# Forgetting attention: the second head of each unit takes its query tiles from long to short, with every projection group in one PSUM bank

## The chip, the cores and the metric

The kernel runs on one core of one Trainium2 chip. The metric is the device time of one execution in microseconds; the median of three runs stands for a kernel.

## What is computed

A decoder block over 1024 tokens of width 1024, in float32: an RMS norm, one wide projection, two kinds of attention, a gated sum of both, an output projection, and then an MLP. The change touches the forgetting attention, eight heads of width 64:

```python
s = jnp.einsum('bqhd,bkhd->bhqk', q_blk, k) * scale
s = s + jnp.transpose(F_blk, (0, 2, 1))[..., None] - F_k
mask = k_pos[None, :] <= q_pos[:, None]
s = jnp.where(mask[None, None], s, NEG_INF)
p = jax.nn.softmax(s, axis=-1)
return jnp.einsum('bhqk,bkhd->bqhd', p.astype(v.dtype), v)
```

The mask is causal. A tile of 128 queries, number i of 8, needs the key tiles 0 to i, that is i + 1 of them. The first query tile is the shortest, with one key tile, and the last is the longest, with eight.

## The kernel before

Every engine has its own instruction list, written out by hand; semaphores tie the lists together. Inputs are split into a high and a low part of float32r, and a projection is three products (high by high, high by low, low by high).

**Units and steps.** The attention is worked in ten units `t` of two heads. Units 0 to 5 are the dilated attention, units 6 to 9 (`N_DIL` to `N_DIL + 3`) the forgetting attention; they are called F0, F1, F2 and F3 here. A unit has 16 steps `s`, one per query tile of one head, and a step's number over the whole program is `G = 16 t + s`. Two steps are a block `B`, with two neighbouring query tiles of one head. `head_of` alternates the heads from block to block. `query_tile` gives both heads their tiles in rising order, so that the number of key tiles runs 1, 2, 1, 2, 3, 4, 3, 4, 5, 6, 5, 6, 7, 8, 7, 8 over the steps 0 to 15.

**What a step does on each engine.**

- TensorE (`mixer_steps`, L1235 on) issues `scores(G)` (L1184) into `PS[G % 2]`, a first part of a projection group (L1141), the transposes of the probabilities of step G - 1 (L1196), and the other two parts of the projection. At odd steps `values` (L1217) of block (G - 3)/2 follows. At the steps 1 and 2, four transposes of the values follow (L1230), which use the same two half banks of `PS[2]` as the transposes of the probabilities.
- VectorE runs `maxes(G)` (L2208: bias and row maximum), the subtraction `probs_lo(G - 1)` (L2215), at even steps `outs` (L2229) ahead of `maxes` and `query_lo` behind it, `values_lo` (L2196) at the steps 1 and 2, and side work: halves of `split_lo` (L2110) for projection weights, `k_stack` (L2181), and at step 7 `normalise` (L2245). In F0 it also merges the dilated groups (L2239).
- ScalarE starts a step with `raw_evacuate` (L1587) for each projection group that ended in the step before, then at even steps `out_part` (L1679), then `query_hi` (L1640), `probs_hi(G - 1)` (L1664), `exps(G)` (L1654), at the steps 1 and 2 `values_hi` (L1647), and last the side work of the step: `split_hi` (L1547) by the table `HI_STEPS` or `k_stack` (L1627) by `K_HI_STEPS`.

The lists are in program order on each engine. So an evacuation at the head of step G stands behind all that ScalarE does in step G - 1, side work included. `HI_STEPS` puts a weight cast at step 2 of F1 and F3 and at step 8 of F1, among others; `K_HI_STEPS` puts a key cast at step 8 of F2.

**Projection groups.** While a forgetting unit is worked, the projections that a later unit needs are computed in between: `group_steps` gives five groups of 24 products to each of F0, F1 and F2, at the steps 0 to 2, 3 to 5, 6 to 8, 9 to 11 and 12 to 15, and four to F3, of four steps each. A group accumulates in a half of one PSUM bank pair. Mostly this is the upper half of `PS[3]`. One group per unit, named in `SECOND_BANK`, takes the upper half of `PS[0]` instead; it lies idle in the steps 0 to 7, where the scores of even steps need at most the lower half. In F0, F1 and F2 that is the group of the steps 3 to 5; in F3 it is the group at the steps 0 to 3, and `scores` waits at step 8 until that bank is emptied. `evacuated(u, g)` says how many evacuations must be done before a group may start (the wait on `raw_out` in `project`, L1138): a group that changes the bank need not wait for the one just before it.

```python
def psp(u, g):
    other = g % 2 if u <= N_DIL else (u, g) in SECOND_BANK.values()
    return (PS[0] if other else PS[3])[:, HALF:2 * HALF]
```

**Around the mixers.** Before F0 stands the combination of the dilated groups. After step 15 of F3 two more steps drain the last block, and then TensorE goes on with the gate projections (L1315), while VectorE and ScalarE start forming the operands of the gate products once the last `values` is done.

Of the kernel before, what the change touches and what calls it, by code (L numbers as in the profile page):

```python
# [32 lines left out]
P = 128  # L33
# [20 lines left out]
N_DIL = 2 * len(DILATIONS)  # L54
# [5 lines left out]
STEPS = 16  # L60
# [133 lines left out]
    return [(u, g) for u, g, steps in group_steps(t) if s == steps[-1]]  # L194


SECOND_BANK = {N_DIL: (N_DIL + 1, 4), N_DIL + 1: (N_DIL + 2, 3), N_DIL + 2: (N_DIL + 3, 2), N_DIL + 3: (N_DIL + 4, 0)}
HI_STEPS = {(N_DIL, 5): 24, (N_DIL, 11): 25, (N_DIL + 1, 2): 26, (N_DIL + 1, 8): 27, (N_DIL + 1, 13): 28,
            (N_DIL + 2, 4): 29, (N_DIL + 2, 10): 30, (N_DIL + 3, 2): 31, (N_DIL + 3, 9): 32}
LO_STEPS = {(N_DIL, 6): (24, 0), (N_DIL, 7): (24, 1), (N_DIL, 13): (25, 0), (N_DIL, 14): (25, 1),  # L200
# [12 lines left out]
    return DILATIONS[t // 2] if t < N_DIL else None  # L213


def query_tile(s):

    return 2 * (s // 4) + s % 2


def head_of(s):

    return s // 2 % 2


def block_keys(B):

    t, b = divmod(B, BLOCKS)
    keys = [[j for j, _ in key_tiles(t, b // 2 * 2 + e)] for e in range(2)]
    both = [j for j in keys[0] if j in keys[1]]  # L230
    order = [(j, (0, 1)) for j in both]
    order += [(j, (e,)) for e in range(2) for j in keys[e] if j not in both]
    return min(keys[0] + keys[1]), order
# [12 lines left out]


def tiles_of(G):
    return key_tiles(G // STEPS, query_tile(G % STEPS))


def units_of(G):
# [18 lines left out]
def pair_view(ap, t):  # L271

    return ap.rearrange("p (r l) -> p r l", r=4) if dil_of(t) == 16 else ap
# [11 lines left out]
def after(eng, sem, n):  # L285

    if n > 0:
        eng.wait_ge(sem, n)


def build(nc, x, g_attn, w_in, b_forget, w_branch, w_out, g_mlp, w_up, w_down, g_final, rope, f_rows, r_rows, x_mid, hidden, sg, out):
# [8 lines left out]
    with ExitStack() as ctx:  # L300
# [101 lines left out]

        def psp(u, g):

            other = g % 2 if u <= N_DIL else (u, g) in SECOND_BANK.values()
            return (PS[0] if other else PS[3])[:, HALF:2 * HALF]

        def evacuated(u, g):

            if u <= N_DIL:  # L410
                return 6 * u + g - (1 if g else 0)
            ends = (u, g) in SECOND_BANK.values() or divmod(6 * u + g - 1, 6) in SECOND_BANK.values()
            return 6 * u + g - (1 if ends else 0)

        pso = PS[3][:, 0:HALF]

# [35 lines left out]
        def stat(G, w):  # L452

            t, s = divmod(G, STEPS)
            if t >= N_DIL:
                c = (t - N_DIL) * STEPS + head_of(s) * 8 + query_tile(s)
                return fox_stat[:, w, c:c + 1]
            c = t % 2 * 2 + head_of(s)
            return dil_stat[:, t // 2 * 8 + query_tile(s), w, c:c + 1]

        def q_raw(t):
            return tmp[:, 2 + t % 2, :]
# [608 lines left out]
        def _(pe):  # L1071
# [84 lines left out]
            def scores(G):  # L1156
                t, s = divmod(G, STEPS)
                h = head_of(s)
                tiles = tiles_of(G)
                if s in (0, 2):  # L1160
                    pe.wait_ge(k_lo, 2 * t + h + 1)
                if G == STEPS * N_DIL + 1:
                    pe.wait_ge(spr_out, 6)
                if t >= N_DIL and s == 8:
                    pe.wait_ge(raw_out, 6 * SECOND_BANK[t][0] + SECOND_BANK[t][1] + 1)
                pe.wait_ge(q_hi, 2 * (G // 2) + 2)
                pe.wait_ge(q_lo, G // 2 + 1)
                after(pe, exp_done, G - 1)
                query = q_st(G // 2)[:, :, G % 2 * P:(G % 2 + 1) * P]
                ps = psc[G % 2]  # L1170
                base = tiles[0][0]
                end = tiles[-1][0] + 1 - base
                for c0 in range(0, end, 4):
                    n = min(4, end - c0)
                    o = ps[:, c0 * P:(c0 + n) * P]
                    kc = slice((base + c0) * P, (base + c0 + n) * P)
                    ops = [(query[:, 0, :], k_st[t % 2][h][:, kc], o),
                           (query[:, 1, :], k_st[t % 2][h][:, kc], o)]
                    for j, mask in tiles:
                        if mask and c0 <= j - base < c0 + n:  # L1180
                            a = (j - base) * P
                            ops.append((ident_b[:], diag_b[:], ps[:, a:a + P]))
                    for m, (lt, rh, oo) in enumerate(ops):
                        ins = pe.matmul(oo, lt, rh, start=(m == 0), stop=(m == len(ops) - 1), skip_group_check=True)  # L1184
                ins.then_inc(qk_done, 1)

            def transposes(G):
                pe.wait_ge(exp_done, G + 1)
                if G % STEPS == 3:
                    pe.wait_ge(v_lo, 2 * (G // STEPS) + 2)  # L1190
                for n, (a, b) in enumerate(units_of(G)):
                    u = units_before(G) + n
                    after(pe, pt_lo, u if G % STEPS in (1, 2) else u - 1)
                    o = tr_bank(G, u)
                    for k in range(a, b):
                        ins = pe.transpose(o[:, (k - a) * P:(k - a + 1) * P],  # L1196
                                           probs(G)[:, k * P:(k + 1) * P], ident[:])
                    ins.then_inc(tr_done, 1)
# [336 lines left out]
        def _(act):  # L1535
# [93 lines left out]
            def query_hi(B, n):  # L1629

                t, b = divmod(B, BLOCKS)
                if n == 0:
                    act.wait_ge(raw_out, 6 * t + 4)
                    if t < N_DIL:
                        act.wait_ge(roped, 16 * t + 16)
                    after(act, qk_done, 2 * B - 2)
                row = 64 * (b % 2)
                dst = row if n == 0 else 64 - row
                cols = slice(b // 2 * 2 * P, (b // 2 + 1) * 2 * P)
                act.activation(q_st(B)[dst:dst + 64, 0, :], q_raw(t)[row:row + 64, cols], ACT.Copy,  # L1640
                               scale=-QSCALE).then_inc(q_hi, 1)

# [453 lines left out]
        def _(dve):  # L2096
# [87 lines left out]
            def query_lo(B):  # L2184
                t, b = divmod(B, BLOCKS)
                row = 64 * (b % 2)
                cols = slice(b // 2 * 2 * P, (b // 2 + 1) * 2 * P)
                dve.wait_ge(q_hi, 2 * B + 1)
                dve.scalar_tensor_tensor(out=q_st(B)[row:row + 64, 1, :], in0=q_raw(t)[row:row + 64, cols], scalar=-QSCALE,
                                         in1=q_st(B)[row:row + 64, 0, :].bitcast(F32),  # L2190
                                         op0=ALU.mult, op1=ALU.subtract).then_inc(q_lo, 1)
# [32 lines left out]
            def outs(B):  # L2224
                t, b = divmod(B, BLOCKS)
                row = 64 * (b % 2)
                dst = og[:, t // 2, (t % 2) * 1024:(t % 2 + 1) * 1024] if t < N_DIL else keep[:, (t - N_DIL) * 1024:(t - N_DIL + 1) * 1024]
                dve.wait_ge(op_done, B + 1)
                dve.tensor_tensor(pair_tokens(dst[row:row + 64], t, b // 2), pair_view(o_bank(B)[row:row + 64, :], t),  # L2229
                                  pair_view(o_part[row:row + 64, :], t), ALU.add).then_inc(on_done, 1)  # L2230

            def merge(n):
# [638 lines left out]
```

## Time and profile before

| | us |
|---|---|
| median of 3 runs | 1572.83 |
| lowest and highest run | 1572.31, 1574.82 |
| the profiled execution, its own time | 1572.4 |
| its span, first to last instruction | 1570.5 |
| TensorE busy | 1509.0 (96%) |
| weight loads of TensorE busy | 1243.4 (79%) |
| VectorE busy | 1092.4 (70%) |
| ScalarE busy | 795.7 (51%) |
| the forgetting units F0 to F3 | 373.5 to 602.5 |

The profile is of one execution. In it, PE is TensorE's products, PEld its weight loads, DVE is VectorE, ACT ScalarE, and SPq the queue that issues DMAs. PEclk is TensorE's granted clock as a share of full speed: 1.00 is 2.4 GHz, 0.50 is 1.2 GHz. In a timeline row, the brackets at the end hold how long the engine had been idle before it, and what released it.

### The profile page before, as it was taken

What the parts mean: (1) busy time and instruction counts of PE and PEld (TensorE: products, weight loads), DVE (VectorE), ACT (ScalarE), POOL (GpSimd) and SP (SyncE); (2) the same over time, 40 slices, a digit from 0 to 9 for tenths busy, and PEclk for the clock granted to TensorE, in tenths of its full rate; (3) what the DMA queues carried; (4) which work ended last, traced back from release to release, by engine and by line L of the source; (5) the groups of instructions that cost most, each with busy time, mean ns of one, the idle gap of its engine ahead of it and who ended that gap; (6) DMA issues with size and microseconds to landing.
All of it is one profiled execution on the core that took longest, in us unless ns stands there. A gap on an engine that the chain in (4) does not pass through costs nothing. (4 is left out here: it accounts for less than half of the span.)

```text
span 1570.5 us, 20831 instructions
## 1 busy us (share of the span) xinstructions
PE 1509.0 (96%) x7364; PEld 1243.4 (79%) x7364; DVE 1092.4 (70%) x1747; ACT 795.7 (51%) x1438; POOL 9.5 (1%) x24
## 2 busy tenths in 40 slices
PE   6999999999999999999999999999999899999997
PEld 5788888876888887788888878888888677777776
DVE  4687777656666768743665676666666887777776
ACT  5577666654777775434134543343334444444442
POOL 1000000000000000000000000000000000000001
PEclk9999999999999999999999999999999999999999
DMA  5211111110121113333645424444446664444402
GB/s 188 95 59 37 41 57 38 41 36 19 40 56 55 28 42 99 90 118 118 210 124 141 135 87 152 164 151 151 148 148 206 243 228 148 147 148 148 148 27 108
DMA packets 168277, 173.40 MB, mean 110 GB/s; under 512 B 7848, under 2 KB 127720, under 8 KB 167792
## 3 DMA queue, kind: packets, MB, share of 16 engines
q1 hardware_dynamic: 168176, 172.07, 33.9%
q8 instruction: 61, 1.00, 0.3%
q14 instruction: 40, 0.33, 0.1%
HBM read 125.84 MB, written 46.20 MB: 110 GB/s over the span
## 5 line engine op out<-in xcount | busy, mean ns | idle before, releaser
L1141 PE MATMUL ps<-hspl,wsp 128*128 128x512 f32 x1536 | 422.0, 407 | 7.3 <-DVE wsp L2110 3.2
L1141 PEld LDWEIGHTS ps<-hspl,wsp 128*128 128x128 f32 x1536 | 265.0, 189 | 53.7 <-issue 6.7
L1498 PE MATMUL ps<-dn_b,a_hi 128*128 128x512 f32 x896 | 279.0, 393 | 17.2 <-DVE keep L2342 11.4
L1498 PEld LDWEIGHTS ps<-dn_b,a_hi 128*128 128x128 f32 x896 | 167.3, 189 | 59.6 <-issue 21.8
L1498 PE MATMUL ps<-dn_b,a_lo 128*128 128x512 f32 x448 | 175.2, 391 | 0.0
L2342 DVE TENSOR_TENSOR keep<-keep,ps 128x512 f32<-128x512 f32 (+1 forms) x144 | 101.5, 713 | 42.3 <-PE ps L1498 23.9
L1498 PE MATMUL ps<-up_b,a_hi 128*128 128x512 f32 x384 | 118.4, 390 | 0.4 <-DVE up_b L2342 0.4
L1958 ACT ACTIVATE keep<-keep 128x512 f32<-128x512 f32 x64 | 40.5, 633 | 125.5 <-DVE keep L2644 42.0
L1498 PEld LDWEIGHTS ps<-dn_b,a_lo 128*128 128x128 f32 x448 | 84.4, 188 | 17.8
L2342 DVE TENSOR_TENSOR dn_b<-dn_raw,dn_b 128x1024 fp32r<-128x1024 f32 x56 | 67.1, 1221 | 39.7 <-ACT dn_b L1974 39.7
L2229 DVE TENSOR_TENSOR keep<-ps,o_part 64x256 f32<-64x256 f32 x80 | 39.7, 496 | 71.7 <-ACT o_part L1679 71.0
L2508 DVE TENSOR_TENSOR a_lo<-a_raw,a_hi 128x1024 fp32r<-128x1024 f32 (+1 forms) x66 | 81.3, 1234 | 11.0 <-ACT a_hi L1924 10.9
L1934 ACT COPY ps<-ps 128x512 f32<-128x512 f32 x46 | 26.3, 571 | 121.7 <-PE ps L1498 120.2
L1498 PEld LDWEIGHTS ps<-up_b,a_hi 128*128 128x128 f32 x384 | 72.1, 188 | 15.7 <-DVE up_b L2342 0.8
L1498 PE MATMUL ps<-up_t4b,a_hi 128*128 128x512 f32 x256 | 80.0, 394 | 2.0 <-issue 2.0
L1664 ACT CAST work<-ps 128x128 fp32r<-128x128 f32 (+3 forms) x144 | 51.1, 366 | 59.3 <-PE ps L1196 58.4
L1498 PE MATMUL ps<-up_t,a_hi 128*128 128x512 f32 x256 | 80.0, 394 | 0.0
L1498 PE MATMUL ps<-up_b,a_lo 128*128 128x512 f32 x192 | 74.7, 389 | 0.0
L1196 PE MATMUL ps<-ident,tmp 128*128 128x128 f32 x428 | 73.1, 273 | 1.6 <-ACT tmp L1654 1.4
L1217 PEld LDWEIGHTS ps<-work 128*128 128x128 f32 x456 | 68.2, 189 | 7.3 <-DVE work L2215 1.5
L1217 PE MATMUL ps<-work 128*128 128x256 f32 (+1 forms) x456 | 69.5, 272 | 1.3 <-DVE work L2215 1.3
L1196 PEld LDWEIGHTS ps<-ident,tmp 128*128 128x128 f32 x428 | 54.0, 140 | 20.0 <-ACT tmp L1654 4.3
(242 smaller groups left out, 2819.8 us busy)
## 6 DMA issues: line engine op xcount, KB each, us to landing
hidden<-keep SPq DMA_DIRECT2D x112, 256.0 KB, 2.2
dn_raw<-hidden SPq DMA_DIRECT2D x56, 512.0 KB, 6.0
raw<-in_w_in SPq DMA_DIRECT2D x35, 512.0 KB, 3.8
a_raw<-in_w_up SPq DMA_DIRECT2D x36, 256.0 KB, 3.1
sgl<-sg SPq DMA_DIRECT2D x8, 1024.0 KB, 5.1
a_raw<-in_w_down SPq DMA_DIRECT2D x32, 256.0 KB, 3.1
spare<-in_w_down SPq DMA_DIRECT2D x32, 256.0 KB, 4.1
spare<-in_w_up SPq DMA_DIRECT2D x28, 256.0 KB, 3.2
```

The lines of the kernel that those rows point to most:

```text
L1141: ins = pe.matmul(psp(u, g), wsp[c % 2][:, wp, k * P:(k + 1) * P], hspl[:, mp, k, cols], start=(n == 0), stop=(n == 23), skip_group_check= ...
L1196: ins = pe.transpose(o[:, (k - a) * P:(k - a + 1) * P], probs(G)[:, k * P:(k + 1) * P], ident[:])
L1217: ins = pe.matmul(o[:, cols], v_nat[:, j, 2 * (b % 2):2 * (b % 2) + 2, :].rearrange("p a d -> p (a d)"), moving, start=(part == 0 and (n = ...
L1498: ins = pe.matmul(o, a_part(n, j, wp, k), b_block(n, j, mp, k), start=(first and k == 0 and m == 0), stop=(k == ks - 1 and m == 2), skip_g ...
L1664: act.copy(pt_tiles(G, 0, a, b), tr_bank(G, u)[:, 0:(b - a) * P].rearrange("p (j c) -> p j c", c=P)).then_inc(pt_hi, 1)
L1934: act.copy(s1[q] if q < 2 else bank_b(q), bank_a(q)).then_inc(s1_ok, 1)
L1958: act.activation(u, u, ACT.Square).then_inc(signal, 1)
L2229: dve.tensor_tensor(pair_tokens(dst[row:row + 64], t, b // 2), pair_view(o_bank(B)[row:row + 64, :], t), pair_view(o_part[row:row + 64, :] ...
L2342: return dve.tensor_tensor(out, a, b, op)
L2508: dve.tensor_tensor(a_lo_t[q % 2][b][:], src[:], a_hi_t[q % 2][b][:].bitcast(F32), ALU.subtract).then_inc(a_lo, 1)
```

## The change

`query_tile` now depends on the unit. For the second head of a forgetting unit the pair of tiles is 3 - s // 4 instead of s // 4, so the number of key tiles over the steps 0 to 15 is 1, 2, 7, 8, 3, 4, 5, 6, 5, 6, 3, 4, 7, 8, 1, 2. `SECOND_BANK` is gone: every projection group of the forgetting units is in the upper half of `PS[3]`, and each waits for the evacuation of the one before it. The wait of `scores` at step 8 goes. Transposes at step 2 have two bank halves now (seven tiles), so the wait for `values_lo` stands at the second half of step 2 as well. The tables of side work are as before. The number of products, casts and subtractions is unchanged.

```diff
-SECOND_BANK = {N_DIL: (N_DIL + 1, 4), N_DIL + 1: (N_DIL + 2, 3), N_DIL + 2: (N_DIL + 3, 2), N_DIL + 3: (N_DIL + 4, 0)}
...
-def query_tile(s):
-
-    return 2 * (s // 4) + s % 2
+def query_tile(t, s):
+
+    pair = 3 - s // 4 if t >= N_DIL and head_of(s) else s // 4
+    return 2 * pair + s % 2
+
+
+def pair_of(B):
+
+    t, b = divmod(B, BLOCKS)
+    return query_tile(t, 2 * b) // 2
...
         def psp(u, g):
 
-            other = g % 2 if u <= N_DIL else (u, g) in SECOND_BANK.values()
+            other = g % 2 if u <= N_DIL else 0
             return (PS[0] if other else PS[3])[:, HALF:2 * HALF]
 
         def evacuated(u, g):
 
             if u <= N_DIL:
                 return 6 * u + g - (1 if g else 0)
-            ends = (u, g) in SECOND_BANK.values() or divmod(6 * u + g - 1, 6) in SECOND_BANK.values()
-            return 6 * u + g - (1 if ends else 0)
+            return 6 * u + g
...
-                if t >= N_DIL and s == 8:
-                    pe.wait_ge(raw_out, 6 * SECOND_BANK[t][0] + SECOND_BANK[t][1] + 1)
...
             def transposes(G):
                 pe.wait_ge(exp_done, G + 1)
-                if G % STEPS == 3:
-                    pe.wait_ge(v_lo, 2 * (G // STEPS) + 2)
+                s = G % STEPS
                 for n, (a, b) in enumerate(units_of(G)):
                     u = units_before(G) + n
-                    after(pe, pt_lo, u if G % STEPS in (1, 2) else u - 1)
+                    if (s, n) in ((2, 1), (3, 0)):
+                        pe.wait_ge(v_lo, 2 * (G // STEPS) + 2)
+                    after(pe, pt_lo, u if (s, n) in ((1, 0), (2, 0)) else u - 1)
...
-                cols = slice(b // 2 * 2 * P, (b // 2 + 1) * 2 * P)
+                cols = slice(pair_of(B) * 2 * P, (pair_of(B) + 1) * 2 * P)
```

**TensorE, unit F1, steps 2 and 3.** The names: `q_fox` and `work` are the queries and keys of the scores, `diag_b` the mask of the diagonal tile, `hspl` and `wsp` the operands of the projection, `ident,tmp` a transpose; the number behind `ps` is the bank pair. Before:

```order
L1184 MATMUL ps0<-work_50,q_fox_59 128x128 x2
L1184 MATMUL ps0<-diag_b,ident_b 128x128
L1141 MATMUL ps3<-hspl_49,wsp0_54 128x512 x2
L1196 MATMUL ps2<-ident,tmp_56 128x128 x2
L1141 MATMUL ps3<-hspl_49,wsp0_54 128x512 x6
L1230 MATMUL ps2<-ident,tmp_56 128x128 x4
L1184 MATMUL ps1<-work_50,q_fox_59 128x256 x2
L1184 MATMUL ps1<-diag_b,ident_b 128x128
L1141 MATMUL ps0<-hspl_49,wsp0_54 128x512 x2
```

and with the change:

```order
L1187 MATMUL ps0<-work_50,q_fox_59 128x512 x2
L1187 MATMUL ps0<-work_50,q_fox_59 128x384 x2
L1187 MATMUL ps0<-diag_b,ident_b 128x128
L1146 MATMUL ps3<-hspl_49,wsp0_54 128x512 x2
L1200 MATMUL ps2<-ident,tmp_56 128x128 x2
L1146 MATMUL ps3<-hspl_49,wsp0_54 128x512 x6
L1234 MATMUL ps2<-ident,tmp_56 128x128 x4
L1187 MATMUL ps1<-work_50,q_fox_59 128x512 x4
L1187 MATMUL ps1<-diag_b,ident_b 128x128
L1146 MATMUL ps3<-hspl_49,wsp0_54 128x512 x2
L1200 MATMUL ps2<-ident,tmp_56 128x128 x7
```

Step 2 has scores over 512 and 384 keys instead of one tile, step 3 over twice 512 instead of 256. The projection products behind the scores of step 3, the start of a new group, write `ps3` like the group before, where they wrote `ps0`.

**ScalarE, unit F1, from the copy of the inverses in step 2 to step 3.** `tmp,fox_stat<-ps` is the exponential, `work<-ps 128x4x2x64` is `values_hi`, `wsp_55<-raw_53` the weight cast, `tmp<-ps` the evacuation. Before:

```order
L1672 COPY inv_rows<-ps 16x128
L1679 COPY o_part<-ps 64x256
L1640 ACTIVATE q_fox<-tmp 64x256
L1664 CAST work<-ps 128x2x128
L1654 ACTIVATE tmp,fox_stat<-ps,fox_stat 128x128
L1647 CAST work<-ps 128x4x2x64
L1547 CAST wsp_55<-raw_53 128x1024
L1587 COPY tmp<-ps 128x512
L1640 ACTIVATE q_fox<-tmp 64x256
```

and with the change:

```order
L1676 COPY inv_rows<-ps 16x128
L1683 COPY o_part<-ps 64x256
L1644 ACTIVATE q_fox<-tmp 64x256
L1668 CAST work<-ps 128x2x128
L1658 ACTIVATE tmp,fox_stat<-ps,fox_stat 128x896
L1651 CAST work<-ps 128x4x2x64
L1551 CAST wsp_55<-raw_53 128x1024
L1591 COPY tmp<-ps 128x512
L1644 ACTIVATE q_fox<-tmp 64x256
L1668 CAST pt_odd<-ps 128x4x128
L1668 CAST pt_odd<-ps 128x3x128
L1658 ACTIVATE tmp,fox_stat<-ps,fox_stat 128x1024
```

The order is the same. The exponential ahead of `values_hi`, the weight cast and the evacuation is over 896 columns instead of 128, and the one in step 3 over 1024 instead of 256.

## Rows read from the trace of the kernel before

**Rows 1.** windows, 373.5 to 602.5 us: PE, PEld, DVE, ACT, POOL; PEclk

```profile
373.50:602.50 229.00, 222.53 (x1356) 187.19 (x1355) 158.01 (x332) 159.15 (x363) 0.00 (x0) 1.00 0.14 40
```

**Rows 2.** what TensorE waited for, 370 to 605 us: total us, times, longest

```profile
PE ps L1141 <- ACT tmp L1587: 2.0, 2, 1.1
...
PE ps L1196 <- ACT tmp L1654: 0.8, 1, 0.8
```

**Rows 3.** timeline, F2, steps 8 and 9: start, us, engine, line [idle before <- releaser]

```profile
516.68 1.04 ACT L1627 CAST work<-tmp 64x1024 fp32r<-64x1024 f32 x1
...
518.38 0.73 PE L1141 MATMUL ps<-hspl,wsp 128*128 128x512 f32 x2 [1.11 <-ACT tmp L1587]
```

**Rows 4.** timeline, unit F1, steps 1 to 3

```profile
437.31 0.62 PE L1230 MATMUL ps<-ident,tmp 128*128 128x128 f32 x4
...
437.69 0.41 PE L1184 MATMUL ps<-work,q_fox 128*128 128x128 f32 x2
...
437.99 0.71 PE L1141 MATMUL ps<-hspl,wsp 128*128 128x512 f32 x2
...
438.59 0.69 DVE L2196 TENSOR_TENSOR work<-ps,work 128x512 fp32r<-128x512 f32 x1 [3.84 <-ACT work L1647]
...
439.31 0.43 DVE L2229 TENSOR_TENSOR keep<-ps,o_part 64x256 f32<-64x256 f32 x1
...
439.77 0.30 DVE L2208 CUSTOM_DVE_ANT_0 ps<-ps,fbias 128x128 f32<-128x128 f32 x1
...
440.21 0.37 ACT L1654 ACTIVATE tmp<-ps,fox_stat 128x128 f32<-128x128 f32 x1 [0.42 <-DVE fox_stat L2208]
...
440.50 0.48 PE L1184 MATMUL ps<-work,q_fox 128*128 128x256 f32 x2
440.79 0.59 ACT L1647 CAST work<-ps 128x512 fp32r<-128x512 f32 x1
...
440.87 0.71 PE L1141 MATMUL ps<-hspl,wsp 128*128 128x512 f32 x2
...
441.27 1.05 ACT L1547 CAST wsp<-raw 128x1024 fp32r<-128x1024 f32 x1
...
442.22 0.59 ACT L1587 COPY tmp<-ps 128x512 f32<-128x512 f32 x1
```

**Rows 5.** groups by form, 373.5 to 602.5 us: busy us, mean ns | idle before

```profile
L2208 DVE CUSTOM_DVE_ANT_0 ps<-ps,fbias 128x1024 f32<-128x1024 f32 x8 | 9.8, 1231 | 0.7 <-PE ps L1184 0.5
...
L1654 ACT ACTIVATE tmp<-ps,fox_stat 128x1024 f32<-128x1024 f32 x8 | 9.0, 1122 | 0.5 <-DVE fox_stat L2208 0.3
L2208 DVE CUSTOM_DVE_ANT_0 ps<-ps,fbias 128x896 f32<-128x896 f32 x8 | 8.8, 1095 | 0.6
...
L1654 ACT ACTIVATE tmp<-ps,fox_stat 128x896 f32<-128x896 f32 x8 | 8.1, 1015 | 0.1
```

**Rows 6.** timeline, unit F3, TensorE at step 14 (seven key tiles)

```profile
589.74 1.03 PE L1184 MATMUL ps<-work,q_fox 128*128 128x512 f32 x4
...
590.65 0.71 PE L1141 MATMUL ps<-hspl,wsp 128*128 128x512 f32 x2
```

**Rows 7.** timeline, unit F0, step 3

```profile
384.18 0.70 PE L1141 MATMUL ps<-hspl,wsp 128*128 128x512 f32 x2 [1.85 <-DVE wsp L2110]
```

**Rows 8.** timeline, unit F3, steps 7 to 9

```profile
568.92 1.23 DVE L2245 TENSOR_TENSOR keep<-keep,tmp 128x1024 f32<-128x1024 f32 x1 [2.73 <-DMA tmp<-r_rows]
...
572.71 0.77 PE L1196 MATMUL ps<-ident,tmp 128*128 128x128 f32 x5 [0.81 <-ACT tmp L1654]
```

**Rows 9.** timeline, the end of the mixers

```profile
600.66 0.39 PE L1217 MATMUL ps<-pt_odd,work 128*128 128x256 f32 x1 [1.56 <-DVE work L2215]
```

**Rows 10.** windows in the MLP, columns as in the first group

```profile
932.00:936.00 4.00, 4.00 (x13) 3.10 (x12) 2.14 (x3) 1.82 (x2) 0.00 (x0) 0.57 0.24 74
936.00:940.00 4.00, 4.00 (x19) 3.29 (x18) 3.79 (x4) 2.24 (x4) 0.00 (x0) 1.00 0.56 169
```

More of the change, by code:

```diff
@@ L228, in block_keys @@
     t, b = divmod(B, BLOCKS)
-    keys = [[j for j, _ in key_tiles(t, b // 2 * 2 + e)] for e in range(2)]
+    keys = [[j for j, _ in key_tiles(t, query_tile(t, 2 * b + e))] for e in range(2)]
     both = [j for j in keys[0] if j in keys[1]]
@@ L248, in tiles_of @@
 def tiles_of(G):
-    return key_tiles(G // STEPS, query_tile(G % STEPS))
+    return key_tiles(G // STEPS, query_tile(G // STEPS, G % STEPS))
 def units_of(G):
@@ L455, in stat @@
             if t >= N_DIL:
-                c = (t - N_DIL) * STEPS + head_of(s) * 8 + query_tile(s)
+                c = (t - N_DIL) * STEPS + head_of(s) * 8 + query_tile(t, s)
                 return fox_stat[:, w, c:c + 1]
             c = t % 2 * 2 + head_of(s)
-            return dil_stat[:, t // 2 * 8 + query_tile(s), w, c:c + 1]
+            return dil_stat[:, t // 2 * 8 + query_tile(t, s), w, c:c + 1]
         def q_raw(t):
@@ L2186, in query_lo @@
                 row = 64 * (b % 2)
-                cols = slice(b // 2 * 2 * P, (b // 2 + 1) * 2 * P)
+                cols = slice(pair_of(B) * 2 * P, (pair_of(B) + 1) * 2 * P)
                 dve.wait_ge(q_hi, 2 * B + 1)
@@ L2228, in outs @@
                 dve.wait_ge(op_done, B + 1)
-                dve.tensor_tensor(pair_tokens(dst[row:row + 64], t, b // 2), pair_view(o_bank(B)[row:row + 64, :], t),
+                dve.tensor_tensor(pair_tokens(dst[row:row + 64], t, pair_of(B)), pair_view(o_bank(B)[row:row + 64, :], t),
                                   pair_view(o_part[row:row + 64, :], t), ALU.add).then_inc(on_done, 1)
```

## The prediction

> **What bounds the kernel now.** The busy table says TensorE, at 96% of the span. The window over the four forgetting units says the same of the place where the change works: 222.5 of 229.0 us busy, at a granted clock of 1.00 [rows 1]. VectorE has 158.0 us of work there and ScalarE 159.2, so neither is near its limit as a sum. The change leaves the number of products, casts and subtractions as it is; it can only move the moments at which TensorE waits. So I read next what TensorE waited for in this stretch. ScalarE's evacuation of a projection group ended two waits [rows 2], one in F1 and one in F2, both at step 9; the timeline of F2 shows why [rows 3]. A key cast of 1.04 us stands on ScalarE behind the exponential of step 8, the evacuation stands behind the cast, and TensorE stands idle for 1.11 us before it can start the next group. F1 has the same picture with a weight cast. Three more waits: 1.85 us in F0 at step 3 for split weights [rows 7], 0.81 us in F3 at step 9 for an exponential [rows 8], and 1.56 us behind the last transposes [rows 9]. All else in the 229 us is TensorE at its own pace. The whole stock that a better order could win back is about 6 us, 0.4% of the time. A measurement of this kernel can tell about 0.2%, or 3.1 us, from no change.
>
> **Where a wait for an evacuation comes from.** A group that starts at an odd step follows an even step, which has no `values` products to pass the time. TensorE needs for it only the rest of the step and the next scores, while VectorE must find the maximum, ScalarE must take the exponential, do its side work, and then evacuate. Before, the groups starting at steps 3 and 6 were free of this by the second bank. Now all wait, and the new order puts seven key tiles on step 2, just ahead of the group that starts at step 3.
>
> **F1, step 3, worked out.** I count from the start of the first value transposes, V = 437.31 [rows 4]. TensorE then takes scores of step 2, which took 0.30 us (437.69 to 437.99) and with seven tiles take 0.91 [rows 6]: 0.61 more. Scores of step 3 took 0.37 (440.50 to 440.87) and have eight tiles: one tile more than the 0.91, so 0.96, 0.59 more. TensorE was ready for the new group at 440.87, V + 3.56, and is now at V + 4.76.
>
> The other engines: VectorE can't start the maximum of step 2 before `outs`, which ended at 439.74 (V + 2.43) and hangs on the value transposes through ScalarE, not on the scores. It started at V + 2.46. Over 896 columns it takes 1.10 us where 128 columns took 0.30 [rows 4, 5]; with 0.08 for reading the result out, it ends at V + 3.64. The exponential takes 1.02 [rows 5] and its read-out 0.1: V + 4.8. `values_hi`, the weight cast and the evacuation follow in order. From the starts at 440.79, 441.27 and 442.22 they stand 0.48 and 0.95 apart, and the evacuation takes 0.59 [rows 4]. So it starts at V + 6.3 and ends at V + 6.85. TensorE resumes at about V + 6.9 and has **waited 2.1 us**.
>
> **F2, step 3.** The table puts no weight cast at step 2, so the 0.95 falls away: **1.15 us**.
>
> **F3** has four groups of four steps, with six products a step instead of eight, about 0.22 us each ([rows 10]: 19 in 4.00 us). No group starts at step 3. But transposes of step 2 now have a second half that waits for `values_lo`. TensorE comes to it at V + 4.76, less two products before, plus two products and four transposes of 0.45 us: V + 5.25. `values_hi` is done at V + 5.4, `values_lo` takes 0.69 [rows 4] and ends at V + 6.15: **0.9 us**. The group at step 4 is next. With three transposes, four products, two short `values` and scores of three tiles, TensorE is ready at V + 8.4. ScalarE has the weight cast of step 2 until V + 6.35, then `query_hi` (0.4) and two casts of about 0.5, until V + 7.8, then the exponential over 1024 columns, 1.12 [rows 5], its read-out, and the evacuation: V + 9.7. **1.3 us**.
>
> **F0, step 3.** TensorE already waits for weights that VectorE splits late. The second half of the split stands behind `values_lo`, so behind maximum and exponential of step 2. Those grow by 0.80 and 0.65 [rows 4, 5], 1.45 together; TensorE itself comes 1.2 later. The wait of 1.85 us [rows 7] grows by **0.3**. The evacuation is done by then and costs nothing.
>
> **The other group starts.** Step 6 follows step 5 with the `values` of the eight-tile block, sixteen products: 1.9 us of cover, enough even for F0's weight cast at step 5. Steps 12 and 0 follow odd steps too. At step 9 the steps 8 and 9 have five and six tiles as before. Only `probs_hi` ahead of the exponential has six tiles instead of four, one cast more (about 0.35), against 0.22 more transposes on TensorE: **0.1 us** each in F0, F1 and F2. If that cover were gone, each would cost the pitch of one cast, 0.5.
>
> **What goes.** F3's wait for the exponential came from `normalise`, which stood 2.73 us for the inverses' DMA at step 7 [rows 8] and held back the maximum of step 8. Between the weight split that releases that DMA and step 7, TensorE now has one long `values` (1.5 more), six more transposes and four more tiles of scores, 2.9 us in all, and the new waits on top: the DMA is in, and the **0.8 to 1.0 us** goes. At the end the last block has one and two tiles. One cast and one subtraction of two tiles stand where there were two of four tiles each; the 1.56 us [rows 9] becomes about 0.9, **0.65 us** less. The gate forms behind it start when the last `values` is done, before and now, so nothing follows there. The four waits of `scores` at step 8 go, but the second bank had long been empty.
>
> **The sum.** Added: 0.3 + 2.1 + 1.15 + 0.9 + 1.3 + 0.3 = 6.05 us. Taken away: 1.0 + 0.65 = 1.65. Net **+4.4 us**. The profiled execution took 1572.4 (a span of 1570.5 and 1.9 around it), so it would take 1576.8; it lies 0.4 below the median, so the median goes to **1577.2 us**, 0.28% slower. Bounds: the new waits are not below nothing; if my chain is long by 0.3 at each of the five places they give 4.5, if short by as much 7.5. That is 1575.7 to 1578.7. The MLP has a few stretches at half clock after waits of its own; one more or one less is 6 products in 4 us [rows 10], about 1.4 us, and a shifted start may make or lose one. Together, the likeliest case spans 1574.5 to 1580.
>
> **Rivals.**
>
> *A, the maximum isn't held up.* If VectorE starts the maximum of step 2 right behind the scores (V + 1.3) and not behind `outs`, the chain is 1.1 us shorter. The waits become 1.05 in F1, 0.1 in F2, and in F3 nothing for the transposes and 0.3 for the group. With 0.6 for the rest that is 2.05, less 1.65: +0.4, 1573.2. Against it: VectorE's list has `outs` first, and it began the maximum of step 2 0.03 us behind it [rows 4]. Chance 0.25, for everything that falls between +3.1 and -3.1.
>
> *B, faster.* The alternation lets ScalarE get ahead: if the exponential of step 8 starts 1.1 us earlier relative to TensorE, the evacuation at step 9 is in time, the 2.0 us of F1 and F2 [rows 2] go as well, and with A the sum is 0.4 - 2.0 - 0.3 = -1.9, 1570.9; it decides at 1.1 us. For it: steps 10 and 11 are lighter, and the long blocks no longer come in a row. Against it: the exponential of step 8 follows its own scores, which the order doesn't move. Chance 0.11.
>
> *C, a backlog.* In F1 the exponential of step 3 ends at about V + 10.25 by the same chain and the transposes that need it come at V + 11.1. If 0.85 us more is lost on the way, it waits there too, in F0 to F3: another 1 us each, +8.4, 1581.2. Chance 0.08.
>
> *D, the clock falls.* In the trace the clock stayed at 1.00 in this stretch, through a wait of 1.85 us [rows 1, 7]. The new waits are of that size, so I keep it there. If it fell behind one of them, 1.4 us more each [rows 10], 1582 with four. Chance 0.03. The Trainium skill (TensorE: Matmul & The Clock Gate, "A second HAM failure mode: psum-queue depth-cycling") says that micro-idles between groups of products, from cycling through PSUM buffers, can let the clock fall again and again; by that rule the time would be that of this rival. The trace so far speaks against it.
>
> **Numbers.** Forecast, C, D and the upper part of the likeliest case: chance of slower by over 0.2% 0.62; within 0.2% 0.27; faster by over 0.2% 0.11. For 8 in 10 the range takes in A and C and reaches nearly to B: 1571.4 to 1581.2.
>
> **What would show it.** In the profile after: TensorE idle at the first projection product of step 3, released by the evacuation, about 2.1 us in F1 and 1.15 in F2, with the weight cast just ahead of it in F1; about 0.9 us inside the transposes of step 2 and 1.3 us at step 4 in F3; F0's wait still named for split weights, near 2.1; step 9 of F1 and F2 as before; no wait of `normalise` for a DMA; about 0.9 us at the end. The four units together go from 229.0 to about 233.4 us. I am wrong if the maximum of step 2 begins before `outs`, if step 9 loses its waits, or if TensorE waits in a place not named here.

## The result

The changed kernel takes 1578.46 us (median of 13 runs, 1572.15 to 1583.34), the kernel before 1573.77 us beside it (13 runs, 1570.71 to 1575.6). The ratio is 1.0027, with a 95% interval of 1.0017 to 1.0038: slower by 2.7 to 6.0 us. Forecast were 1577.2 us and +4.4 us. The profiled execution took 1580.04 us, with a span of 1578.1 and a mean granted clock of 0.991, where the one before had 0.995.

**The window over the four units**, columns as in [rows 1], up to the first gate product:

```profile
373.50:607.60 234.10, 224.43 (x1356) 188.95 (x1355) 158.55 (x332) 159.52 (x363) 0.00 (x0) 0.99 0.14 39
```

It has grown from 229.0 us to 234.1, with the same 1356 products; 233.4 were forecast. Against [rows 1] the granted clock reads 0.99 and not 1.00; what that cost is told below. The spans of the two profiled executions differ by 7.6 us; the 2.5 beyond the 5.1 lie behind the four units, where the clock fell in places of its own (near 635 us, and for 6.8 us instead of 3.4 near 922).

**What TensorE waited for** in the changed kernel (total us, times, longest), against [rows 2]:

```profile
PE ps L1146 <- ACT tmp L1591: 5.4, 5, 1.7
PE ps L1146 <- DVE wsp L2114: 2.3, 1, 2.3
PE ps L1221 <- DVE work L2219: 1.1, 1, 1.1
PE ps L1200 <- DVE work L2200: 0.5, 1, 0.5
PE ps L1200 <- DVE work L2219: 0.4, 1, 0.4
```

Evacuations (L1591) now end five waits instead of two, 5.4 us instead of 2.0. The split weights (L2114) are F0's wait. The wait for the exponential in F3 [rows 8] is gone from the list, and one new kind has come, for `values_lo` (L2200). Transposes that wait for `probs_lo` (L2219) stood in the list of before too, with 0.3 us in F0; that one is gone, and this one is in F1.

**F1, steps 2 and 3**, the place that the prediction works out. V is 438.98 here, the start of the value transposes; the timeline's columns are those of [rows 4]:

```profile
440.98 0.43 DVE L2233 TENSOR_TENSOR keep<-ps,o_part 64x256 f32<-64x256 f32 x1
...
441.44 1.10 DVE L2212 CUSTOM_DVE_ANT_0 ps<-ps,fbias 128x896 f32<-128x896 f32 x1
...
442.68 1.01 ACT L1658 ACTIVATE tmp<-ps,fox_stat 128x896 f32<-128x896 f32 x1 [1.04 <-DVE fox_stat L2212]
...
443.68 0.57 ACT L1651 CAST work<-ps 128x512 fp32r<-128x512 f32 x1
...
443.83 0.23 PE L1187 MATMUL ps<-diag_b,ident_b 128*128 128x128 bf16 x1
444.14 1.05 ACT L1551 CAST wsp<-raw 128x1024 fp32r<-128x1024 f32 x1
...
445.09 0.59 ACT L1591 COPY tmp<-ps 128x512 f32<-128x512 f32 x1
...
445.74 0.73 PE L1146 MATMUL ps<-hspl,wsp 128*128 128x512 f32 x2 [1.68 <-ACT tmp L1591]
```

The maximum over 896 columns starts right behind `outs`, at V + 2.46, as worked out; the exponential runs from V + 3.70, `values_hi`, weight cast and evacuation follow 0.46 and 0.95 apart, and TensorE, which ended the scores with the mask product of 443.83, starts the group at V + 6.76 (V + 6.9 was forecast). The profile calls it idle for 1.68 us. Matmul rows overlap, so idle time read off them is a little short; measured from start to start, less the usual spacing of the same pair of products, the wait is 1.87 us. All waits below are given that way, and those under 0.2 us are left out of the table. The forecasts are the prediction's; where it gave a growth (F0's step 3, and step 9) it is added to the wait before.

| place | before | after | forecast for after |
|---|---|---|---|
| F0 step 2, `probs_lo` | 0.44 | 0 | not listed |
| F0 step 3, weights | 2.04 | 2.51 | 2.34 |
| F1 step 3, evacuation | 0 | 1.87 | 2.1 |
| F2 step 3, evacuation | 0 | 0.94 | 1.15 |
| F1, F2 step 9, evacuation | 1.05, 1.31 | 1.09, 1.35 | 1.15, 1.41 |
| F1 step 15, `probs_lo` | 0 | 0.59 | 0 |
| F3 step 3, `values_lo` | 0 | 0.65 | 0.9 |
| F3 step 4, evacuation | 0 | 1.08 | 1.3 |
| F3 step 9, an exponential | 0.98 | 0 | 0 |
| end of the mixers, `probs_lo` | 1.56 | 1.07 | 0.9 |

The last row is the idle time of the profile. The waits sum to 7.38 us before and 11.15 after, 3.8 us more. The stretch has grown by 5.1 us. The rest comes from this (a window as above, in F0's step 3):

```profile
386.00:389.00 3.00, 3.00 (x12) 2.60 (x11) 1.66 (x4) 1.75 (x3) 0.00 (x0) 0.50 0.63 175
```

Right behind F0's wait TensorE's clock stood at 0.50, 1.2 GHz, for 3.4 us, from 385.9 to 389.3; 12 products took the 3 us of the window. Steps of projection products were spaced 0.43 us instead of 0.23, and F0's step 3 lost 1.7 us to it. (3.8 and 1.7 are 0.4 us more than the growth; that remainder was not traced.) In the profile before there was no such fall here. It is rival D, once, in this execution.

### The profile page after: what moved, and what is told of

It is laid out like the page before. It is cut to its first block and busy times, and to the rows that moved or that the text cites. A ratio compares the mean times of both kernels' runs of the same rounds, so it can differ in the third digit from the quotient of the medians.

```text
span 1578.1 us, 20831 instructions
## 1 busy us (share of the span) xinstructions
PE 1513.7 (96%) x7364; PEld 1247.5 (79%) x7364; DVE 1092.8 (69%) x1747; ACT 796.6 (50%) x1438; POOL 9.5 (1%) x24
## 5 line engine op out<-in xcount | busy, mean ns | idle before, releaser
L2219 DVE TENSOR_TENSOR work<-ps,work 128x128 fp32r<-128x128 f32 (+3 forms) x144 | 58.5, 415 | 18.2 <-ACT work L1668 17.6
```

The lines of the kernel that those rows point to most:

```text
L2219: dve.tensor_tensor(pt_tiles(G, 1, a, b), tr_bank(G, u)[:, 0:(b - a) * P].rearrange("p (j c) -> p j c", c=P), pt_tiles(G, 0, a, b).bitcast ...
```

## The experiments

Nine kernels, each timed in five rounds beside the kernel before. Ratios are to that kernel, with their 95% intervals.

**x1: the bank without the order.** Of the changed kernel, only the reversal is taken back:

```diff
-    pair = 3 - s // 4 if t >= N_DIL and head_of(s) else s // 4
+    pair = s // 4
```

> Both heads take their tiles from short to long as before, but every group is in one bank and waits for the evacuation before it. My theory: the wait hangs on ScalarE's queue, so it is there in the old order too. At step 3 TensorE is ready at V + 3.56; the evacuation ends at V + 5.5 in F1 (behind the weight cast) and 0.95 earlier in F2: waits of 1.95 and 1.0 us, nothing new at step 6. F0 keeps its 1.85 us for weights. Time 3.0 us above before, between before and the change. Rival (it is the long block at step 2 that makes the evacuation late, the bank alone costs nothing): no new wait at step 3, time as before. Transposes of step 14 in F1, which waited 0.6 us in the change, do not wait here.

Measured: 1577.29 us, ratio 1.0019 (1.0009 to 1.0028). Of TensorE's wait list over the units:

```profile
PE ps L1146 <- ACT tmp L1591: 5.7, 6, 1.8
PE ps L1146 <- DVE wsp L2114: 1.9, 1, 1.9
```

And of its timeline, F1's step 3 (the weight cast, the evacuation, the group):

```profile
441.49 1.05 ACT L1551 CAST wsp<-raw 128x1024 fp32r<-128x1024 f32 x1
...
442.43 0.59 ACT L1591 COPY tmp<-ps 128x512 f32<-128x512 f32 x1
...
443.07 0.73 PE L1146 MATMUL ps<-hspl,wsp 128*128 128x512 f32 x2 [1.80 <-ACT tmp L1591]
```

With one key tile at step 2 TensorE still waits for the evacuation: 1.99 us in F1 (behind the same weight cast) and 1.05 in F2. The rival falls, and the transposes of step 14 in F1 do not wait here, as expected. What makes the group at step 3 wait is the shared bank; the long block ahead of it is not needed. TensorE is then ready earlier and ScalarE too, and the difference stays. Step 9 of F1 and F2 waits as before (1.05, 1.31). Two waits were not expected, 0.71 us at step 6 of F0 and 0.73 at step 4 of F3. In both, a group start follows a step with short `values`; in F0 a weight cast on ScalarE stands in the way as well. The changed kernel has no wait at F0's step 6: its order puts sixteen `values` products at step 5, as the prediction said. At step 4 of F3 it has a larger one (1.08).

**x2: the order with the second bank in F0, F1 and F2.** There the group of steps 3 to 5 goes back to the upper half of `PS[0]`, with a wait for the exponential that last reads it. F3 keeps its groups in one bank:

```diff
+SECOND_BANK = {N_DIL: (N_DIL + 1, 4), N_DIL + 1: (N_DIL + 2, 3), N_DIL + 2: (N_DIL + 3, 2)}
...
                     after(pe, raw_out, evacuated(u, g))
+                    for tt, group in SECOND_BANK.items():
+                        if (u, g) == group:
+                            pe.wait_ge(exp_done, STEPS * tt + 3)
...
+                if t in SECOND_BANK and s == 6:
+                    pe.wait_ge(raw_out, 6 * SECOND_BANK[t][0] + SECOND_BANK[t][1] + 1)
```

> The changed order, but in F0, F1 and F2 the group of steps 3 to 5 is in the upper half of PS[0] again; it waits only for the exponential of step 2, and the scores of step 6 wait for its evacuation. My theory: TensorE is ready at V + 4.76 and that exponential is done at V + 4.8, so the waits at step 3 of F1 (1.87 in the change) and F2 (0.94) fall to 0.1 each; F0 keeps its wait for weights; the wait at step 6 is covered by the long values. Time 2.6 us below the change, about 1.5 above before. Rival (the long block ahead of the group makes TensorE wait whatever the bank): the waits stay above 1 us.

Measured: 1574.91 us, ratio 1.0009 (0.9998 to 1.002), 3.6 us below the change's median, where 2.6 was expected. Of TensorE's wait list over the units:

```profile
PE ps L1151 <- ACT tmp L1598: 3.0, 3, 1.2
PE ps L1151 <- DVE wsp L2121: 2.3, 1, 2.3
```

Three waits for evacuations are left of five: step 9 of F1 and F2 (1.09, 1.35) and step 4 of F3. Those at step 3 of F1 and F2, 2.8 us together, are gone. So the exponential of a seven-tile step is in time for TensorE, and everything that ScalarE does behind it up to the end of the evacuation is what TensorE waited for.

**x3: the casts moved.** The changed kernel with three entries of ScalarE's tables one step later, and VectorE's subtractions (`LO_STEPS`, `K_LO_STEPS`) with them:

```diff
-HI_STEPS = {(N_DIL, 5): 24, (N_DIL, 11): 25, (N_DIL + 1, 2): 26, (N_DIL + 1, 8): 27, (N_DIL + 1, 13): 28,
+HI_STEPS = {(N_DIL, 5): 24, (N_DIL, 11): 25, (N_DIL + 1, 3): 26, (N_DIL + 1, 9): 27, (N_DIL + 1, 13): 28,
...
-            (N_DIL + 1, 3): (26, 0), (N_DIL + 1, 4): (26, 1), (N_DIL + 1, 9): (27, 0), (N_DIL + 1, 10): (27, 1),
+            (N_DIL + 1, 4): (26, 0), (N_DIL + 1, 5): (26, 1), (N_DIL + 1, 10): (27, 0), (N_DIL + 1, 11): (27, 1),
...
-K_HI_STEPS = {N_DIL: (3, 4), N_DIL + 1: (6, 10), N_DIL + 2: (6, 8)}
-K_LO_STEPS = {N_DIL: (4, 5), N_DIL + 1: (11, 12), N_DIL + 2: (9, 10)}
+K_HI_STEPS = {N_DIL: (3, 4), N_DIL + 1: (6, 10), N_DIL + 2: (6, 9)}
+K_LO_STEPS = {N_DIL: (4, 5), N_DIL + 1: (11, 12), N_DIL + 2: (10, 11)}
```

> The changed kernel with ScalarE's side work moved one step later where it stood ahead of a group that starts at an odd step: weight cast of F1 from step 2 to 3 and from 8 to 9, key cast of F2 from 8 to 9, their subtractions one step later too. My theory (the evacuation is late by what stands ahead of it on ScalarE): the wait at step 3 of F1 falls from 1.87 to about 0.95, as in F2, and the waits at step 9 from 1.1 and 1.35 to 0.1 to 0.3; sum about 3 us below the change, within 1.5 us of before. Rival (the exponential or the maximum sets the wait): they stay as they are, time as the change.

Measured: 1573.23 us, ratio 0.9997 (0.9985 to 1.0008). Of TensorE's wait list over the units:

```profile
PE ps L1146 <- ACT tmp L1591: 2.4, 3, 0.9
PE ps L1146 <- DVE wsp L2114: 2.3, 1, 2.3
```

And of its timeline, F1's step 3 (`values_hi`, the evacuation, the group):

```profile
443.41 0.57 ACT L1651 CAST work<-ps 128x512 fp32r<-128x512 f32 x1
...
443.87 0.60 ACT L1591 COPY tmp<-ps 128x512 f32<-128x512 f32 x1
...
444.52 0.73 PE L1146 MATMUL ps<-hspl,wsp 128*128 128x512 f32 x2 [0.77 <-ACT tmp L1591]
```

In F1 the evacuation follows `values_hi` directly, and the wait is 0.96 us, one cast less. The two waits at step 9 are down to 0.15 us each, as expected. 3.05 us of waits are taken away, and the medians fell by 5.2. The clock has a part in that: over the runs its mean is 0.9942 here and 0.9925 in the change, which goes with 2.3 us by the figure worked out under "The clock" below.

**x4: the order in F3 alone.** F0, F1 and F2 as before:

```diff
-    pair = 3 - s // 4 if t >= N_DIL and head_of(s) else s // 4
+    pair = 3 - s // 4 if t == MIX - 1 and head_of(s) else s // 4
```

(with `SECOND_BANK` back for the first three units, and with it the wait of `scores` at step 8).

> The changed order in F3 alone; F0, F1 and F2 as before with their second bank. My theory: F3 pays 0.65 us in the transposes of step 2 and 1.1 us at step 4, and gets back 0.98 us at step 9 and about 0.65 us at the end, so time is as before within 0.5 us; the granted clock does not fall at 385 us, as F0's wait is the old one. Rival (the gain at the end of the mixers is larger or smaller than the waits it takes): over 1.5 us off before in either direction.

Measured: 1574.81 us, ratio 0.9999 (0.999 to 1.0009). The waits in F3 are 0.65 and 1.07 us, step 9 is free, and in the timeline the end of the mixers stands thus, for [rows 9]:

```profile
601.49 0.39 PE L1225 MATMUL ps<-pt_odd,work 128*128 128x256 f32 x1 [1.07 <-DVE work L2223]
```

The idle time at the end is 1.07 us, 0.49 less than before, not the 0.65 that were forecast. Gains and costs in F3 cancel within the error: 1.7 us of waits have come, 1.5 are gone, and the ratio is 0.9999. One expectation failed: the clock did fall here at 383.4 us, behind F0's old wait of 2.04 us, and so it did in x1. Of the fall near 384 us the change is not the only author.

**x5 and x6: both orders, mended.** x5 is the new order with x2 and x3 joined, the weight cast of F1's step 13 at step 14, and F0's side work rearranged. x6 is the kernel before, order and banks as they were, with the casts of F1 and F2 moved from step 8 to 9, F3's `normalise` from step 7 to 9, and the same rearrangement, which splits F0's late weights one step earlier (x6 against the kernel before; the first three changes of it are in x3 too):

```diff
-HI_STEPS = {(N_DIL, 5): 24, (N_DIL, 11): 25, (N_DIL + 1, 2): 26, (N_DIL + 1, 8): 27, (N_DIL + 1, 13): 28,
+HI_STEPS = {(N_DIL, 5): 24, (N_DIL, 11): 25, (N_DIL + 1, 2): 26, (N_DIL + 1, 9): 27, (N_DIL + 1, 13): 28,
...
-K_HI_STEPS = {N_DIL: (3, 4), N_DIL + 1: (6, 10), N_DIL + 2: (6, 8)}
-K_LO_STEPS = {N_DIL: (4, 5), N_DIL + 1: (11, 12), N_DIL + 2: (9, 10)}
+K_HI_STEPS = {N_DIL: (3, 4), N_DIL + 1: (6, 10), N_DIL + 2: (6, 9)}
+K_LO_STEPS = {N_DIL: (4, 5), N_DIL + 1: (11, 12), N_DIL + 2: (10, 11)}
...
-                if t == N_DIL and s in (0, 1):
-                    jobs += [lambda: merge(2 * s), lambda: merge(2 * s + 1)]
-                if t == N_DIL and s == 2:
-                    jobs += [lambda: split_lo(CH0 + 23, 0), lambda: split_lo(CH0 + 23, 1)]
+                if t == N_DIL and s == 0:
+                    jobs += [lambda: merge(0), lambda: merge(1)]
+                if t == N_DIL and s == 1:
+                    jobs += [lambda: merge(2), lambda: split_lo(CH0 + 23, 0), lambda: split_lo(CH0 + 23, 1)]
+                if t == N_DIL and s == 2:
+                    jobs += [lambda: None, lambda: merge(3)]
-                if t > N_DIL and s == 7:
+                if t > N_DIL and s == (9 if t == MIX - 1 else 7):
```

> The changed order with the second bank for the group of steps 3 to 5 (as x2), the three casts one step later (as x3), the weight cast of F1's step 13 at step 14, and in F0 the weight split done in step 1 and the fourth merge at the end of step 2. My theory: the waits of F1 and F2 at step 3, at step 9 and F1's at step 15 go (1.87 + 0.94 + 1.09 + 1.35 + 0.59, less some 0.3 left over), F0's falls from 2.5 to about 0.8. Time 7 us below the change, 2 to 3.5 below before. Rival (mending one wait makes another, as TensorE's next demand finds VectorE behind): 3 us or less below the change.

> The kernel before with its order and second bank, and only side work moved: the casts of F1 and F2 from step 8 to 9, the weight split of F0 into step 1 with the fourth merge at the end of step 2, normalise of F3 from step 7 to 9. My theory: the waits go that stood there before (1.05, 1.31, 2.04, 0.98), up to 0.5 left over in all: time 4.5 to 5 us below before, and below x5, since the old order has no wait of its own at step 3. The clock has no wait left at 384 us to fall behind. Rival (the new order wins once its waits are mended, by its short last block): x5 below x6.

Measured: x5 1571.31 us, ratio 0.9977 (0.9966 to 0.9987); x6 1569.46 us, ratio 0.997 (0.9955 to 0.9985). Both beat both kernels by what was expected (x5 is 7.2 us below the change, x6 4.7 below before), and x6 is the better by 1.9 us in the medians. The wait list over the units, of x5:

```profile
PE ps L1228 <- DVE work L2226: 1.1, 1, 1.1
PE ps L1151 <- ACT tmp L1598: 0.9, 1, 0.9
PE ps L1207 <- DVE work L2226: 0.8, 1, 0.8
PE ps L1151 <- issue: 0.5, 1, 0.5
PE ps L1207 <- DVE work L2207: 0.5, 1, 0.5
PE ps L1194 <- ACT tmp L1598: 0.3, 1, 0.3
PE ps L1207 <- ACT tmp L1665: 0.2, 1, 0.2
```

And of x6:

```profile
PE ps L1217 <- DVE work L2215: 1.6, 1, 1.6
PE ps L1196 <- ACT tmp L1654: 0.6, 1, 0.6
PE ps L1196 <- DVE work L2215: 0.3, 1, 0.3
```

In x6 no wait of over 0.2 us for an evacuation or for weights is left; 0.43, 0.29 and 0.76 us remain in F0, at steps 2, 5 and 7. In x5 F3's two waits stand (0.65, 1.08), 0.72 is left at F0's step 3, and F0 has three new ones, 0.41, 1.01 and 0.45 us at the steps 4 to 6. By its timeline, the first comes from the maximum over eight tiles, which stands behind a merge of 1.22 us on VectorE; the second from `probs_lo`, which stands behind a key subtraction of 1.22; the third is `scores` waiting for the second bank's evacuation, which stands behind a weight cast of 1.03 on ScalarE. So the order gives 0.49 us at the end, and its waits in F0 and F3 take back more.

**x7: the early split alone, in the changed kernel.** Of the rearrangement above only F0's part:

```diff
-                if t == N_DIL and s in (0, 1):
+                if t == N_DIL and s == 0:
...
+                if t == N_DIL and s == 1:
+                    jobs += [lambda: merge(2), lambda: split_lo(CH0 + 23, 0), lambda: split_lo(CH0 + 23, 1)]
...
-                    jobs += [lambda: split_lo(CH0 + 23, 0), lambda: split_lo(CH0 + 23, 1)]
+                    jobs += [lambda: None, lambda: merge(3)]
```

> The changed kernel with F0's weight split in step 1 and the fourth merge at the end of step 2, nothing else. My theory: the weights are no longer late, and the wait at step 3 of F0 is then set by the evacuation, as in F1 and F2: 1.7 instead of 2.5 us; time 0.8 us below the change, and up to 1.5 more where the clock no longer falls behind that wait. Rival (F0's wait was for weights alone): the wait goes, 2.5 us below the change.

Measured: 1577.87 us, ratio 1.0016 (1.0005 to 1.0028). In its timeline, F0's step 3 and step 5:

```profile
384.55 0.73 PE L1146 MATMUL ps<-hspl,wsp 128*128 128x512 f32 x2 [1.47 <-ACT tmp L1591]
...
392.73 0.52 PE L1200 MATMUL ps<-ident,tmp 128*128 128x128 f32 x3 [0.59 <-DVE work L2219]
```

As expected, F0's wait is now one for the evacuation, and 1.66 us long instead of 2.51. The rival falls: under the late weights the late evacuation had been hidden. But 0.76 us has come up at step 5, the price of moving VectorE's work into the steps before. The gain in waits is 0.1 us, and the median is 0.6 below the change. Up to 1.5 us more was expected if the clock no longer fell there. The profile shows no fall near 384 us, and the mean clock over the runs is 0.9939 against 0.9925, but the time did not follow.

**x8: the early split alone, in the kernel before**, with the same lines as x7, in the old order and the old banks.

> The kernel before with one edit: F0's weight split in step 1 and the fourth merge at the end of step 2. My theory of the clock: it falls near 384 us in some executions because TensorE idles there (2.04 us); with that wait gone no profile of this kernel falls there, and the waits change by -2.04 and about +1.0 at steps 5 and 7 of F0 (as x6 shows: 0.29 and 0.76). Time 1 to 1.5 us below before, with the time at half clock in the mean of the runs up to 2 us less. Rival (the clock's falls don't depend on this wait): a fall near 384 us stays.

Measured: 1570.55 us, ratio 0.9974 (0.9961 to 0.9987). The mean of its 12 runs is 3.3 us below the mean of the 81 runs of before that the nine experiments had beside them, and 4.0 below the 17 of its own session (the interval is 2.0 to 6.1). Expected were 1 to 1.5. F0's wait of 2.04 is gone, and 0.31 and 0.74 us have come at steps 5 and 7; step 9 of F3 waits 0.85 instead of 0.98. In waits that is 1.1 us. The profiled execution, the fastest of the 12, has no fall of the clock near 384 us. That decides nothing, since the profile of before has none there either. The mean granted clock over the runs is 0.9948 against 0.9934 (0.9928 in its own session).

**x9: two key subtractions later, in x6.**

```diff
-K_LO_STEPS = {N_DIL: (4, 5), N_DIL + 1: (11, 12), N_DIL + 2: (10, 11)}
+K_LO_STEPS = {N_DIL: (8, 10), N_DIL + 1: (11, 12), N_DIL + 2: (10, 11)}
```

> x6 with VectorE's two key subtractions of F0 at steps 8 and 10 instead of 4 and 5. My theory: the waits left in x6, 0.29 and 0.76 us at steps 5 and 7 of F0 for an exponential, come from VectorE's backlog behind the merges and these subtractions (1.22 each), so both go: 1 us below x6, 5.5 below before. Rival (they come from ScalarE's key casts at steps 3 and 4): they stay, time as x6.

Measured: 1567.53 us in 5 runs, ratio 0.9951 (0.9934 to 0.9968). Its wait list over the units:

```profile
PE ps L1217 <- DVE work L2215: 1.6, 1, 1.6
PE ps L1196 <- DVE work L2215: 0.3, 1, 0.3
PE ps L1196 <- ACT tmp L1654: 0.2, 1, 0.2
```

Of the two waits the one at step 7 fell from 0.76 to 0.32 us; the one at step 5 stayed, 0.30. So VectorE's backlog made a part of the wait at step 7. For the one at step 5 the timeline of x9 shows the rival, ScalarE's key cast of step 3 (the cast, `out_part`, `outs`, the maximum, the exponential):

```profile
384.59 1.03 ACT L1627 CAST work<-tmp 64x1024 fp32r<-64x1024 f32 x1
...
385.64 0.37 ACT L1679 COPY o_part<-ps 64x256 f32<-64x256 f32 x1
...
386.05 0.42 DVE L2229 TENSOR_TENSOR keep<-ps,o_part 64x256 f32<-64x256 f32 x1 [1.74 <-ACT o_part L1679]
...
386.39 0.55 DVE L2208 CUSTOM_DVE_ANT_0 ps<-ps,fbias 128x384 f32<-128x384 f32 x1
...
387.03 0.58 ACT L1654 ACTIVATE tmp<-ps,fox_stat 128x384 f32<-128x384 f32 x1 [0.18 <-DVE fox_stat L2208]
```

VectorE stood idle for 1.74 us until `out_part`, which starts when the key cast ends, and the maximum follows. No run moved that cast. x9 is the fastest kernel of the study, 7.9 us below the runs of before beside it in the medians.

## Why the prediction was right

**The direction, the size and the place held.** +4.4 us was forecast; the interval is 2.7 to 6.0. The likeliest case is what happened, with some of rival D in it. That the total comes so close is partly luck: the waits grew by 3.8 us and not by 4.4, and a lower clock, of which the forecast had nothing, made up for the difference.

**The chain behind step 2 held, and its waits were forecast some 0.2 us too long.** The maximum starts behind `outs`, as said and against rival A; the new waits at step 3 of F1 and F2 and in F3 measured 1.87, 0.94, 0.65 and 1.08 us for 2.1, 1.15, 0.9 and 1.3. The error is some 0.2 in all four and has two halves, read in F1. The release comes 0.14 earlier, V + 6.76 for V + 6.9: `values_hi` starts 0.1 before the exponential's read-out has ended, where the prediction put one behind the other. And TensorE is ready 0.13 later, V + 4.89 for V + 4.76: the scores of step 3 took 1.06 us, from 442.81 to 443.87, where 0.96 had been put together from [rows 6] and a tile more. F2 is the same to 0.05. In F3's group the release is 0.4 earlier than forecast (V + 9.28 for V + 9.7) and TensorE 0.2 earlier: the longer the chain of durations that was added up, the more it was too long.

**F0's wait was sized right** (2.51 for 2.34). The 0.44 us at its step 2 went, which was not listed. It is back in x1, without the order; the likely reason, the longer scores of step 2 that give VectorE time for `probs_lo`, was not tested by itself. The 0.1 us put down for each step 9 came to 0.05 or less. Against rival B, step 9 of F1 and F2 waits as before: what it waits for follows the scores of step 8, which the order doesn't move.

**What goes was right.** F3's 0.98 us went. `normalise` no longer waits for its DMA. The end gave 0.49 us, the forecast 0.65.

**Missed: F1's step 15**, 0.59 us. It is where the prediction said that it would be wrong, a wait in no named place. After the eight tiles of step 13 the transposes of step 14 have one tile and come early, and need the bank half that the second subtraction of step 13 still reads. The cast ahead of that subtraction stands behind the weight cast of step 13 in ScalarE's list. A short step after a long one lets TensorE run into a backlog that a long step would have covered. In x1, without the order, the wait is gone; so it is in x5, with the order and that weight cast at step 14. x5 has other edits, but none at these steps.

**The clock.** The forecast held it at 1.00 in this stretch and gave its fall a chance of 0.03. It fell there in the profile, once, and cost 1.7 us where rival D had 1.4. (Four falls of 1.4 would have made 1582.8, not the 1582 of the prediction.) Each of 191 timed runs of the eleven kernels lists its mean granted clock. Taken about the mean of its own kernel, 0.001 less clock goes with 1.34 us more time, and this takes the scatter of a kernel's runs from 2.2 to 1.3 us. The mean clock of the change is 0.9925 over 13 runs, of before 0.9934 over 81: 1.2 us of the 3.8 us by which their means differ. The other 2.6 us stand against 3.8 us of waits. The same for all kernels, against before: the waits over the four units in the one profile of each, and the mean time with the clock's part taken out in this way.

| kernel | waits | time at before's clock |
|---|---|---|
| the change | +3.8 | +2.6 |
| x1 | +3.7 | +2.6 |
| x2 | +1.0 | +1.4 |
| x3 | +0.7 | 0.0 |
| x4 | +0.2 | -0.6 |
| x5 | -2.0 | -1.8 |
| x6 | -4.1 | -3.8 |
| x7 | +3.7 | +3.8 |
| x8 | -1.1 | -1.4 |
| x9 | -4.6 | -5.2 |

The times are uncertain by 0.3 to 0.7 us (one standard error). They follow the waits to within 1.2 us in all ten. Together with the runs that took single waits away, that shows the waits to be the cause. The change and x1 are the two that are off most. Part of that may be the gate products behind the mixers, where a wait of 2.19 us was only 0.61 in the profile after. TensorE had been at half clock just ahead of it, from 635 us on, and so arrived later at operands that VectorE was still making. That is one pair of profiles, and the difference stays open.

**Which part of the change costs.** x1, the bank alone, has 3.7 us of waits more than before, nearly all of the change's 3.8. x2, the order with one bank in F3 only, has 1.0 more, and its time can't be told from before (0.9998 to 1.002). The order is close to neutral, the one bank is the cost.

## What to carry over

When a buffer is shared, look in the consumer's own list for what stands between the work that TensorE covers and the release, and count side work in it: here a cast of 1.05 us in the wrong step cost TensorE 0.9 us twice and 1.2 us once (x3). Moving two casts and a job off the steps ahead of such releases, and splitting F0's weights a step earlier, made both orders faster than before, and the old one (x6, 1569.46 us) more than the new one (x5, 1571.31). Here, where TensorE does the waiting, reordering long and short steps mostly moved its waits, while an earlier release took them away.

## Not expected of the hardware

**The clock falls behind some waits, and not every time.** The profiles show a fall near 384 us, in F0's step 3 or just behind it, where TensorE had waited 2.04 us (x1, x4) or 2.51 (the change, x2, x3): five of the six kernels with such a wait there. The kernel before, with 2.04, has none in its profile. The kernels with 0.72 and 1.66 us there, or no wait (x5, x7, x6, x8, x9), have none. The changed kernel's waits of 1.87 and 1.35 in F1 and F2 were not followed by one. A rival was not tested: x1 to x4, which all fell, ran in one session on one chip, and x5 to x9, which did not, in two others on other chips. Against it, the kernel before had a mean clock of 0.9936 beside x1 to x4, and 0.9935 and 0.9928 in the others. The window over x1's fall, with 0.52 where the changed kernel's has 0.50:

```profile
384.00:387.00 3.00, 3.00 (x11) 2.36 (x11) 0.98 (x3) 1.38 (x3) 0.00 (x0) 0.52 0.36 107
```

**Whether one early wait is dear is not shown.** x8 takes 1.1 us of waits away and 3.3 us of time. By the pooled 1.34 us, its clock of 0.9948 against 0.9934 is 1.8 us of it. The kernel's time at half clock in the mean of the runs (one less the clock, doubled, times the time) is 16.5 us in x8, 20.9 before and 23.8 in the change. That fits a fall that follows the wait of 2 us in some executions and not without it. But x2 and x3, with a wait of 2.5 us and a fall in their profiles, have mean clocks of 0.9937 and 0.9942, as high as x7 and x5 without a fall (0.9939 and 0.9941). Nor does the early wait explain the scatter of the change's runs, 11.2 us from fastest to slowest: in x8, without that wait, it is 10.4. Profiles of many executions of x8 and of before, with the falls near 384 us counted, would decide it.
